# Six places for the halves of the weights, moved to six different start points within 256 bytes

## The reference, cut to what is computed

```
block 1: x = LN(a*x + 0.5*swiglu(x));  x = LN(a*x + mixer1(x));  x = LN(a*x + 0.5*swiglu(x))
block 2: x = x + norm(mixer2(norm(x)));  x = x + norm(conv_gelu_ffn(norm(x)))
block 3: x = x + g1*mixer3(norm(x)*(1+s1)+h1);  x = x + g2*(relu(norm(x)*(1+s2)+h2 @ w1)^2 @ w2);  out = norm(x)
```

## The kernel before, in words

| tensor | start point |
|---|---|
| ring, x_high, x_low, w_high (three), w_low (three) | 0 |
| cols (per-partition vectors of the model) | 0 |
| the stages' activations, branch outputs y, f1d_in, c2d_in, f1d_place, c2d_place | 0 |
| f1s_unit, f2s_unit, f3s_unit | 16 |
| f1s_sh, f1s_sl and their like of f2s, f3s | 48 |
| const | 48 |

## Time and profile before

### The profile page before, as it was taken

One profiled execution on the slowest core, in us unless ns is written; L12 is line 12 of the kernel. 1 busy time (PEld: TensorE's weight loads), 2 busy tenths in 40 slices (PEclk: granted clock), 3 DMA queues, 4 the chain that ended last, 5 costly groups with the idle time before them and its releaser, 6 DMA issues. The chain is left out here.

```text
span 3420.3 us, 48737 instructions
## 1 busy us (share of the span) xinstructions
PE 3348.4 (98%) x18576; PEld 2856.2 (84%) x18576; DVE 2278.8 (67%) x3709; ACT 1593.4 (47%) x2932; POOL 339.6 (10%) x375
## 2 busy tenths in 40 slices
PE   8999999999999999999999999999999999999999
PEld 7998888877788899887887888888787888889987
DVE  6887474778447787853565576667465567678865
ACT  3565254454433455555324363346355243355654
POOL 1000200022010100022010100000000104222200
PEclk9999999999999999999999999999999999999999
DMA  6346312220334435520454242245410330142464
GB/s 218 109 149 206 111 49 64 91 69 25 104 102 137 157 108 170 173 73 25 160 161 143 75 134 97 96 165 168 122 38 26 109 99 26 38 148 81 136 200 157
DMA packets 107988, 386.48 MB, mean 113 GB/s; under 512 B 12060, under 2 KB 14764, under 8 KB 107504
## 3 DMA queue, kind: packets, MB, share of 16 engines
q1 hardware_dynamic: 101088, 364.86, 32.6%
q0 software_dynamic: 4528, 16.43, 1.5%
q10 hardware_dynamic: 2144, 2.10, 0.2%
HBM read 379.13 MB, written 4.21 MB: 112 GB/s over the span
## 5 line engine op out<-in xcount | busy, mean ns | idle before, releaser
L445 DVE TENSOR_TENSOR w_low<-ring,w_high 128x1024 fp32r<-128x1024 f32 (+1 forms) x481 | 591.3, 1231 | 496.3 <-ACT w_high L433 490.6
L433 ACT ACTIVATE w_high<-ring 128x1024 fp32r<-128x1024 f32 (+1 forms) x481 | 485.0, 1010 | 491.8 <-PE bank L469 212.8
L469 PE MATMUL bank<-x_low,w_high 128*128 128x512 f32 (+1 forms) x1712 | 654.9, 388 | 19.5 <-DVE w_low L445 13.0
L469 PE MATMUL bank<-x_high,w_low 128*128 128x512 f32 (+1 forms) x1712 | 641.4, 380 | 0.0
L469 PE MATMUL bank<-x_high,w_high 128*128 128x512 f32 (+1 forms) x1712 | 417.8, 381 | 0.0
L469 PEld LDWEIGHTS bank<-x_low,w_high 128*128 128x128 f32 x1712 | 323.1, 189 | 82.4 <-issue 17.6
L469 PEld LDWEIGHTS bank<-x_high,w_low 128*128 128x128 f32 x1712 | 323.4, 189 | 56.9 <-issue 3.6
L469 PEld LDWEIGHTS bank<-x_high,w_high 128*128 128x128 f32 x1712 | 304.6, 189 | 59.1 <-issue 4.8
L738 PE MATMUL bank<-w_low,x_high 128*128 128x512 f32 (+1 forms) x384 | 145.6, 379 | 3.6 <-ACT z_z L2102 1.5
L740 PE MATMUL bank<-w_high,x_high 128*128 128x512 f32 (+1 forms) x384 | 143.5, 374 | 0.0
L739 PE MATMUL bank<-w_high,x_low 128*128 128x512 f32 (+1 forms) x384 | 143.5, 374 | 0.0
(11 more groups left out here) (821 smaller groups left out, 8215.0 us busy)
## 6 DMA issues: line engine op xcount, KB each, us to landing
ring<-in_W SPq DMA_DIRECT2D x686, 512.0 KB, 3.5
X<-in_x POOLq DMA_DIRECT2D x1, 2048.0 KB, 9.7
x_spill<-X POOLq DMA_DIRECT2D x1, 2048.0 KB, 8.2
X<-x_spill POOLq DMA_DIRECT2D x4, 512.0 KB, 3.5
ring<-in_W SPq DMA_DIRECT2D x4, 432.0 KB, 4.0
out<-X SPq DMA_DIRECT2D x3, 512.0 KB, 5.5
const<-in_consts POOLq DMA_DIRECT2D x1, 1133.0 KB, 10.6
f_hid<-in_xT ACTq DMA_DIRECT2D x4, 256.0 KB, 8.2
```

Of the source, the lines that this page charges most:

```text
L433: ac.activation(b.UH[u.place][:, 0:u.K * u.n], u.src(), ACT.Copy).then_inc(*b.split.act.up("high", i))
L445: dv.tensor_tensor(b.UL[u.place][:, 0:n], u.src(), b.UH[u.place][:, 0:n].bitcast(F32), SUB).then_inc(*b.split.dve.up("low", i))
L469: i = pe.matmul(out, w[:, k, c], v, start=n == 0 and q == 0, stop=last and q == 3 * K - 1)
```

## The change

```diff
-        self.colt = a.take("cols", self.ncol)
+        self.colt = a.take("cols", self.ncol, past=3 * LINE)
...
-        self.UH = [a.take("w_high", SLOT, dtype=F32R) for _ in range(NU)]
-        self.UL = [a.take("w_low", SLOT, dtype=F32R) for _ in range(NU)]
+        self.UH = [a.take("w_high", SLOT, dtype=F32R, past=n) for n in (4, 8, 12)]
+        self.UL = [a.take("w_low", SLOT, dtype=F32R, past=n) for n in (16, 32, 48)]
```

## The result

| | us |
|---|---|
| before, median of 2 runs | 3423.38 (3421.72 to 3425.03) |
| after, median of 2 runs | 3459.86 (3459.70 to 3460.02) |
| ratio, 95% interval | 1.0101 (1.0080 to 1.0122) |
| span of the profiled execution, before and after | 3420.3 and 3458.6 (+38.3) |

The kernel became slower by 36.5 us. The forecast was +14.8 us: its direction was right, its range (3410 to 3478 us) held the time, and its size was 21.7 us too small.

What follows compares the result with a forecast made beforehand. TensorE, busy 3348.4 of 3420.3 us, was taken as the bound. Terms of 6.3 + 6.4 - 1.5 + 3.6 = +14.8 us gave a span of 3435.1 and, with 3.1 for the runs' median, 3438.2 us; range 3410 to 3478.

Steps and rivals of the forecast that it cites:

- Item 2: 512 columns, weights stationary, 1832 triples with x or a branch's y: 3.5 ns slower a triple, +6.4 us.
- Item 1: 512 columns, weights moving, 896 triples of L738 and L852: 7 ns slower a triple, +6.3 us.
- Item 4: 256 columns, sums of x at 48 moving, 720 triples: a passing cost of 20 ns at each of 180 products, +3.6 us.
- Item 3: 256 columns, x moving, triples of L469 and of product 4: 2 ns faster on 768 matmuls, -1.5 us.
- Items 5 and 6: VectorE's splits and ScalarE's writes, and the rest (x shifted by 256 bytes, stages' tensors, DMAs): 0 each.
- Every sign that the prediction gave for being right: c2d triples 685 to 700 ns apart; products 6, 5, 7, 3 over 1.36 us; 256-column tiles 117 to 120 ns.
- nothing: Rival: the moving tensor's own start point may set the levels, or address has no effect; 3423 us, chance 0.30.
- Faster: Rival: operands starting in the same part of 256 bytes clash, and the change separates them; 3413 us, chance 0.14.
- Off a 64-byte multiple: Rival: w_high at 4, 8, 12 costs 7 ns on two matmuls of every triple, 54 us; 3478 us, chance 0.14.

Runs made afterwards that it cites:

- e3: The changed kernel with all six weight places (three w_high, three w_low) at start point 16: 3463.39 us, ratio 1.0107.
- e6: The changed kernel with all six weight places back at 0 and x_high and x_low at start point 48 instead: 3443.43 us, ratio 1.0055.
- e5: The changed kernel with all six weight places back at 0, so that only cols and the small tensors stay moved: 3424.57 us, ratio 1.0000.
- e8: The changed kernel with all six weight places at start point 32: 3463.49 us, ratio 1.0117.
- e1: The changed kernel with the three w_high back at 0, the three w_low still at 16, 32 and 48: 3449.02 us, ratio 1.0067.
- e9: The kernel before with x_high and x_low at start point 48 in the three MLP stages and their added place at 0: 3422.78 us, ratio 0.9993.
- e12: e9 with the added place at 0 in the first MLP only and at 16 in the other two: 3418.91 us, ratio 0.9984.

## Why the prediction was right in direction and wrong in size

The mechanism was right: TensorE is the bound, nothing but the distance between matmuls can change, and stationary and moving operand disturb each other by their start points. The three terms that cost time were sized too small; no bound that it gave was passed.

- **Item 2 is the step that failed.** "512 columns, weights stationary" was put at 3.5 ns a triple, 6.4 us. It measured 3.8 ns a matmul with x and 4.6 with y, 11 to 14 a triple, +20.5 us, 14.1 more than forecast, where the whole was off by 21.7. The row that it was taken from was of 256 columns, x past weights at 16 and at 0 (118 and 120 ns). That row could not carry the conclusion: distance 16 has two levels there, the row stood in the upper one (e3 has the same products with the same start points in the lower), and at 256 columns distance 0 is itself a slow one, so that the difference from it says nothing of 512 columns, where 0 is the best. The 512-column rows with moving weights were the nearer ones: the law is the same whichever operand moves. The prediction named this as what would make it wrong, and it did.
- **Item 1** was forecast at 7 ns a triple, 6.3 us, and measured 12 to 14.7 (c2d's triples, 680, became 693.3, 696.3 and 695.0 in the three places), +10.7 us. The steady 685 of the earlier trace rows was a distance of 48, by e3 and e6 the cheapest of all those off 0; 16, 32 and 60 cost two to three times that.
- **Item 4** was forecast at the passing cost of product 6, 20 ns a product, 3.6 us. It measured 4.2 ns a matmul, 50 ns a product, +9.0 us: what was read as a cost of the passage was, for the new start points, the steady state. This group was the only one at the 256-column floor; its distance was 16, the only one at which whole groups met that floor. And 113 was not a property of its start points, as the first round of the same stage shows (117.8).
- **Item 3** was forecast at -1.5 us and measured -0.9. 120 went to 118 at the tiles, not to 113.
- **Items 5 and 6**, 0, held: splits at 1227 against 1226, gaps shorter by 2.3 us, and e5 at a ratio of 1.0000.

Every sign that the prediction gave for being right came: c2d's triples at 693 to 696 ns in the mean of each place, products 6, 5, 7 and 3 at 1.40 us and more, the tiles at 118, the split within 10 ns. None of them looked at item 2, the largest group, which stood only in the sentence on what would make the prediction wrong. They confirm the mechanism and could not have told the size.

Of the rivals, "nothing" is refuted: 256-column x-moving matmuls did stay near 118, but x moving at 0 past displaced weights costs 3.8 ns at 512 columns, and e6 shows that the moving operand's own point is not what decides. "Faster" is refuted: the clash is not between equal start points, they are the best at 512 columns. "Off a 64-byte multiple" is refuted by e3 and e8, which cost 1.0107 and 1.0117 with everything on 64 bytes; the +36.5 us lie in its band, above 30, and not in the forecast's of 5 to 30, but for another reason than its own: three matmuls of a triple pay some 4 ns each, not two of them 7.

## What to carry to other kernels

Where TensorE is the bound, look at the distance from start to start of neighbouring matmuls by shape, and compare it with the smallest that this shape shows anywhere in the trace; here 4 to 5 ns of 227 on some eight thousand matmuls were 31 of the 36 us. Give stationary and moving operands of 512 fp32r columns the same start point within 256 bytes, and change the layout of one only together with the other. Price an unseen pair from rows of the same number of columns, whichever operand moves there, and not from another shape. Before a level is tied to a pair of addresses, look at the same matmuls in several rounds and stages: the first round here stood at the other level.

## What the runs showed of the hardware

- For 512 columns the pace of these fp32r matmuls depends on the difference of two start addresses within 256 bytes, not on either: 226.8 to 227.8 ns at a distance of 0, 229.1 to 229.3 at 48 floats, and 231.7 to 233.3 at 4, 16, 32 and 60. Why 48 costs less than 16 is open.
- 256 columns have another order: 113 to 114 ns at 16, 118 to 120 in groups at one other distance. Among matmuls of distance 16 others reach the floor as well: in e1 product 7 of the second MLP takes 113.3 ns in every matmul, though its w_low is not at that distance from the sums.
- At 256 columns and distance 16 two levels, 113 and 118 ns, exist for the same start points, and a stretch keeps its own until a longer distance or another pair breaks it (e9: the first MLP in the lower, the others in the upper but for their ends; e12's trace agrees on the first). What picks the level at a break is open; no run varied the moment of entry alone, and each kernel has one trace.
- A matmul with equal start points among others that differ is slowed: in e1, 226.9 and 227.8 ns became 230.2 and 231.3.
- VectorE's split and ScalarE's copy show next to nothing of such a dependence: for f1s_t the split takes 1217 to 1228 ns at start points 16, 32 and 48 against 1214 to 1228 at 0, and ScalarE's copy a median of 1055 at 4, 8 and 12 against 1052 at 0, 3 ns that TensorE's waits do not show.
- Not tried: all places at one of the start points between 16 and 48 other than 32, and x at two start points within the mixers, where the 256-column tiles would want 16 and the 512-column ones 0.
